# An inference step of a hybrid decoder: last experts' products re-ordered, an eleventh expert piece loaded ahead

## The reference

```python
def mixer_output_and_ffn(x, ya, yb, ym, w_out, g_ffn, w_rg, w_re, w_gate, w_up, w_down):
    mixed = jnp.concatenate([ya..., yb..., ym...], axis=-1)
    h = x + jnp.einsum("bsc,cd->bsd", mixed, w_out)
    return h + hier_moe(rms_norm(h, g_ffn), w_rg, w_re, w_gate, w_up, w_down)

def hier_moe(n, w_rg, w_re, w_gate, w_up, w_down):
    # top-1 of 4 expert groups, then top-2 of 8 experts in that group, softmax over the two
    hg = jnp.einsum("nd,edf->nef", t, w_gate)      # 32 experts, d = 2048, f = 256
    hu = jnp.einsum("nd,edf->nef", t, w_up)
    act = jax.nn.silu(hg) * hu * gates[..., None]
    return jnp.einsum("nef,efd->nd", act, w_down)
```

## Time and profile before

| what | value |
|---|---|
| median of 3 executions | 1140.29 us (1138.39 to 1141.09) |
| the profiled execution's own time | 1141.11 us |
| its span, first to last instruction | 1139.2 us |
| mean granted TensorE clock | 0.985 of full speed |
| TensorE busy (matmul) | 1050.7 us, 92% |
| VectorE busy | 550.0 us, 48% |
| ScalarE busy | 200.1 us, 18% |
| read from HBM | 375.63 MB |

### The profile page before, as it was taken

One profiled execution on the slowest core, in us unless ns is written; L12 is line 12 of the kernel. 1 busy time (PEld: TensorE's weight loads), 2 busy tenths in 40 slices (PEclk: granted clock), 3 DMA queues, 4 the chain that ended last, 5 costly groups with the idle time before them and its releaser, 6 DMA issues.

```text
span 1139.2 us, 17257 instructions
## 1 busy us (share of the span) xinstructions
PE 1050.7 (92%) x7153; PEld 585.5 (51%) x7153; DVE 550.0 (48%) x1079; ACT 200.1 (18%) x457; POOL 41.7 (4%) x39
## 2 busy tenths in 40 slices
PE   8999999999999999999999998999997969787976
PEld 3687776666666676677777442333332313232322
DVE  3775554664455455495442135544443434343423
ACT  1022112221212231312010112121211111111110
POOL 0031010000100000010000000000000000000000
PEclk9999999999999999999999999999999999999997
DMA  9899449899999999724856368999999999999993
GB/s 327 329 287 323 185 142 417 319 372 348 350 409 390 375 358 361 295 97 158 336 201 243 148 267 356 417 425 426 427 427 428 427 429 429 427 429 427 427 427 135
DMA packets 38612, 384.53 MB, mean 338 GB/s; under 512 B 4863, under 2 KB 7551, under 8 KB 10207
## 3 DMA queue, kind: packets, MB, share of 16 engines
q1 hardware_dynamic: 35968, 375.83, 82.1%
q0 software_dynamic: 1568, 5.62, 1.9%
q10 hardware_dynamic: 1008, 2.10, 0.5%
HBM read 375.63 MB, written 7.90 MB: 337 GB/s over the span
## 4 chain that ended last, share of the span: by engine, by line
PE 71%; DMA 16%; DVE 8%; ACT 2%; issue 2%; POOL 1%; SPq 0%; ACTq 0%; DVEq 0%; POOLq 0%
PE ps L605 24%; DMA arena<-w_gu 12%; PE ps L597 7%; PE ps L1024 6%; PE ps L1001 5%; PE ps L1055 5%; PE ps L1039 4%; DMA arena<-w_proj 4%; PE ps L798 4%; PE ps L587 3%; PE ps L765 3%; DVE cst L1802 1%; PE ps L1060 1%; DVE cst L1741 1%; PE ps L781 1%
## 5 line engine op out<-in xcount | busy, mean ns | idle before, releaser
L605 PE MATMUL ps<-arena 128*128 128x256 f32 x1456 | 332.9, 383 | 1.0 <-DVE arena L1345 1.0
L605 PEld LDWEIGHTS ps<-arena 128*128 128x128 f32 x1456 | 270.5, 190 | 51.0 <-issue 14.4
L1024 PE MATMUL ps<-arena,cst 128*32 128x512 f32 x1024 | 122.8, 614 | 32.7 <-DMA arena<-w_gu 31.0
L1802 DVE STREAM_TRANSPOSE cst<-ps 128x512 f32<-128x512 f32 x31 | 22.2, 717 | 173.7 <-PE ps L1001 173.7
L597 PE MATMUL ps<-arena 128*64 128x256 f32 x832 | 101.3, 385 | 0.0
L1001 PE MATMUL ps<-arena,cst 128*32 128x512 f32 (+1 forms) x768 | 94.0, 603 | 0.0
L1024 PEld LDWEIGHTS ps<-arena,cst 128*32 128x32 f32 x1024 | 32.1, 112 | 118.2 <-issue 81.2
L1039 PE MATMUL ps<-arena,stat 128*32 128x512 f32 x512 | 66.6, 640 | 23.8 <-DVE stat L1806 23.8
L597 PEld LDWEIGHTS ps<-arena 128*64 128x64 f32 x832 | 55.1, 136 | 37.8 <-issue 14.2
L1824 DVE COPY arena<-ps 32x512 f32<-32x512 f32 x64 | 44.2, 691 | 45.8 <-PE ps L1039 44.5
L1055 PE MATMUL ps<-arena,cst 128*128 128x512 f32 x128 | 57.0, 598 | 9.4 <-ACT cst L1275 9.4
(11 more groups left out here) (264 smaller groups left out, 978.4 us busy)
## 6 DMA issues: line engine op xcount, KB each, us to landing
arena<-w_gu SPq DMA_DIRECT2D x64, 2048.0 KB, 29.2
arena<-w_dn SPq DMA_DIRECT2D x32, 2048.0 KB, 27.5
arena<-w_proj SPq DMA_DIRECT2D x43, 1024.0 KB, 7.7
arena<-kc SPq DMA_DIRECT2D x16, 2048.0 KB, 10.7
arena<-vc SPq DMA_DIRECT2D x16, 2048.0 KB, 9.4
arena<-w_o SPq DMA_DIRECT2D x16, 1024.0 KB, 4.9
arena<-kc SPq DMA_DIRECT2D x8, 1024.0 KB, 8.3
arena<-vc SPq DMA_DIRECT2D x8, 1024.0 KB, 9.8
```

Source lines behind the costliest of these rows:

```text
L605: last = mm(psum[:, regions(v)[j - 1]], left[a], right[:, a], start=first and opens and a == 0, stop=final and a == 1, skip_group_check=True)
L1024: last = mm(ps[g:g + 32, 0, :], xgT[:, s % 2, kt, :], w[:, k, :], start=kt < 4, stop=kt >= KT - 4)
```

## The change

- The kernel asks for 8192 bytes of dynamic DMA scratch per partition, and `arena` grows from 49152 to 51200 floats per partition, by 8192 bytes.
- Piece 0 gets a place used once, behind the pieces 6 and 7: over the later `y4`, the routing's old scratch and `fresh` (sums of the output projection), which moves to the new end. Its load waits for `h_ready` 9, the last use of `fresh`. The ring's indices shift by one, so pieces 0 to 10 are issued before any piece is used; piece 11 waits for two used pieces, and from 11 on each piece waits for the same count as before.
- The routing's small tensors move to `gv` and to constants no longer used; the comparison `cmpb` is made in two halves through one smaller tensor.
- In the last body the second spreading is re-ordered. The weights' transposes and copies are made in the last block but one (`early_turns`), those of the last block's rows also at the partitions of their tile. Products of the first three blocks of `y4` (96 rows) with tile 0 are made before the last block's rows exist (`early_products`), at three places; `yres` of the small tile is put into PSUM by a product with the identity (`rows_first`). When the last block's rows are there, ScalarE copies them once (`y_last`), four products of 32 rows finish tile 0 (`last_tiles`), the small tile is finished and copied by ScalarE, and tile 1 follows. Each tile is stored in two halves of its columns.

```diff
@@ -132,7 +132,7 @@
...
-ARENA = 49152
+ARENA = 51200
...
@@ -221,13 +221,14 @@
...
-fresh = area(A_S + D + 512, 4, HALF)
-once = {6: A_N2, 7: A_N2 + PIECE}
+A_LATE = A_S + 2 * D
+fresh = area(A_LATE, 4, HALF)
+once = {0: A_S + D, 6: A_N2, 7: A_N2 + PIECE}
...
-    return u if u < 6 else (u - 2) % RING
+    return u - 1 if u < 6 else (u - 3) % RING
...
@@ -238,12 +239,13 @@
...
+y_last = area(A_S, COLS)
+pw_last = area(A_S + COLS, NT)
...
-squares = area(A_S + D, COLS)
...
@@ -278,36 +280,39 @@
...
-R0 = A_S + D
-mx = area(R0, 3, 8)
...
-pickb = area(R0 + 1168, 2, 3, 32)
...
-cmpb = area(R0, NMORE, 32)
...
+squares = part
...
+E0 = A_I + 132
+mx = field(gv, E0, 3, 8)
...
+L0, NPART = done + 6 * P + 512, NMORE // 2
+top = field(cst, L0, 3, 8)
...
+pickb = pick
+cmpb = field(cst, L1, NPART, 32)
...
@@ -530,30 +536,32 @@
...
         if o in (1, 3, 5):
-            piece(o // 2, 0)
+            piece(1 + o // 2, o // 5)
         if o in (7, 9):
...
         if o == 11:
-            piece(3, 1)
+            piece(4, 1)
+    sp.wait_ge(h_ready, 9)
+    piece(0, 0)
     sp.wait_ge(unit_done, UNITS_M + UNITS_X + 45)
-    piece(4, 1)
+    piece(5, 1)
     sp.wait_ge(unit_done, UNITS_M + UNITS_X + 48)
-    piece(5, 1)
     piece(8, 2)
+    piece(9, 3)
     sp.wait_ge(logits, 1)
-    piece(9, 3)
-    for u in range(10, 3 * BODY + 10):
+    piece(10, 3)
+    for u in range(11, 3 * BODY + 11):
         sp.wait_ge(piece_used, u - 9 if u < 16 else u - 7)
...
         for j in range(count):
-            u = j + 10
+            u = j + 11
             if j == 0 or u % 3 == 0:
                 e = sp.value_load(eblk_i[0:1, ds(i * BODY + u // 3, 1)], min_val=0, max_val=NEXP - 1)
-            sp.wait_ge(piece_used, i * (3 * BODY) + (j + 3))
+            sp.wait_ge(piece_used, i * (3 * BODY) + (j + 4))
             if u % 3 < 2:
...
@@ -564,11 +572,22 @@
...
-    pieces(last, 3 * BODY - 10)
-    for t, (r0, m) in enumerate(ROWS):
-        sp.wait_ge(added[t], last * 8 + 8)
-        sp.dma_start(o_y[r0:r0 + m, :], yres[0:m, t]).then_inc(y_stored_out, 16)
-    sp.wait_ge(y_stored_out, 48)
+    pieces(last, 3 * BODY - 11)
+    def store(t, h):
+        r0, m = ROWS[t]
+        cols = slice(h * D // 2, (h + 1) * D // 2)
+        sp.dma_start(o_y[r0:r0 + m, cols], yres[0:m, t, cols]).then_inc(y_stored_out, 16)
+    for h in range(2):
+        sp.wait_ge(added[0], last * 8 + (6 + 2 * h))
+        store(0, h)
+    for h in range(2):
+        sp.wait_ge(small_out, 2 * h + 2)
+        store(2, h)
+    for h in range(2):
+        sp.wait_ge(added[1], last * 8 + (6 + 2 * h))
+        store(1, h)
+    sp.wait_ge(y_stored_out, 96)
...
@@ -1007,15 +1026,65 @@
...
-            pe.wait_ge(ring_loaded[u], 16)
+            pe.wait_ge(ring_loaded[u - 1], 16)
...
-            pe.wait_ge(ring_loaded[(u - 2) % RING], i * 48 + 16 * ((u - 2) // RING + 1))
+            pe.wait_ge(ring_loaded[(u - 3) % RING], i * 48 + 16 * ((u - 3) // RING + 1))
+    def early_turns(i):
+        pe.wait_ge(added[1], i * 8 + 4)
+        pe.wait_ge(added[2], i * 8 + 4)
+        pe.wait_ge(pw_made, i * 2 + 2)
+        for t, (r0, m) in enumerate(ROWS):
+            last = tr(ps[:, 4, r0:r0 + m], pw[0:m, t, :], ident[0:m, 0:m])
+        last.then_inc(pwt_mm, 1)
+        for t, (r0, m) in enumerate(ROWS):
+            for g in range(4):
+                last = mm(ps[32 * g:32 * g + 32, 5, r0:r0 + m], pw[0:m, t, 96:128], ident[0:m, 0:m], start=True, stop=True)
+        last.then_inc(pwl_mm, 1)
+    def early_products(i, ns):
+        for n in ns:
+            mm(ps[:, 4 + n, :], pwT[0:96, 0:P], y4[0:96, 512 * n:512 * n + 512], start=True, stop=False)
+    def rows_first(i, n):
+        for j in range(2):
+            cols = slice(1024 * n + 512 * j, 1024 * n + 512 * j + 512)
+            mm(ps[64 * j:64 * j + 64, 1 - n, :], ident[0:64, 0:64], yres[0:64, 2, cols], start=True, stop=False)
+    def last_tiles(i):
+        pe.wait_ge(yl_ready, 1)
+        for n in range(4):
+            mm(ps[:, 4 + n, :], pw_last[32 * n:32 * n + 32, 0:P], y_last[32 * n:32 * n + 32, :],
+               start=False, stop=True).then_inc(comb_mm, 1)
+        pe.wait_ge(ye_copied, i * (4 * BODY) + 4 * (BODY + 1))
+        for k in range(2):
+            for j in range(2):
+                cols = slice(1024 * k + 512 * j, 1024 * k + 512 * j + 512)
+                last = mm(ps[64 * j:64 * j + 64, 1 - k, :], pwT[:, 2 * P:NT], y4[:, cols], start=False, stop=True)
+            last.then_inc(small_mm, 1)
+        for n in range(4):
+            if n >= 2:
+                pe.wait_ge(added[0], i * 8 + (4 + n - 1))
+            mm(ps[:, 2 + n, :], pwT[:, P:2 * P], y4[:, 512 * n:512 * n + 512], start=True, stop=True).then_inc(comb_mm, 1)
...
+            ends = final and s == BODY - 1
...
+                if final and s == BODY - 2 and h:
+                    early_turns(i)
+                if ends and h:
+                    rows_first(i, 0)
+                    pe.wait_ge(pwl_ready, 1)
+                    pe.wait_ge(pwt_ready, i * 2 + 2)
+                    pe.wait_ge(ye_copied, i * (4 * BODY) + 4 * BODY)
+                    early_products(i, [0])
...
@@ -1026,10 +1095,14 @@
...
                 gather((b + 1) % BATCH, i * 2 + (2 + (s + 1) // BATCH))
+            if ends:
+                early_products(i, [1])
             pe.wait_ge(gu_copied, i * BODY + (s + 1))
...
             last.then_inc(ht_mm, 1)
+            if ends:
+                rows_first(i, 1)
             pe.wait_ge(act_ready, i * BODY + (s + 1))
...
@@ -1039,7 +1112,10 @@
...
             last.then_inc(piece_used, 1)
-            if b < BATCH - 1:
+            if ends:
+                early_products(i, [2, 3])
+                last_tiles(i)
+            if b < BATCH - 1 or ends:
                 continue
...
@@ -1258,14 +1334,29 @@
...
-    def experts(i, first):
+    def experts(i, first, final):
...
+            if final and s == BODY - 2:
+                act.wait_ge(pwt_mm, i * 2 + 2)
+                act.wait_ge(pwl_mm, 1)
+                copy(pwT, ps[:, 4, 0:NT]).then_inc(pwt_ready, 1)
+                copy(pw_last, ps[:, 5, 0:NT]).then_inc(pwl_ready, 1)
...
+            if final and s == BODY - 1:
+                copy(y_last, ps[:, 3, :]).then_inc(yl_ready, 1)
+                act.wait_ge(yl_ready, 1)
+                for g in range(2):
+                    copy(y4[96:128, 512 * g:512 * g + 512], y_last[32 * g:32 * g + 32, :]).then_inc(ye_copied, 1)
+                for n in range(2):
+                    act.wait_ge(small_mm, n + 1)
+                    for j in range(2):
+                        copy(yres[0:64, 2, 1024 * n + 512 * j:1024 * n + 512 * j + 512], ps[64 * j:64 * j + 64, 1 - n, :]).then_inc(small_out, 1)
+                continue
...
@@ -1782,9 +1873,10 @@
...
-    link(V.tensor_tensor(cmpb, incl.unsqueeze(1).to_broadcast([P, NMORE, 32]),
-                         iota[:, 0:NMORE].unsqueeze(2).to_broadcast([P, NMORE, 32]), ALU.is_le))
-    link(V.tensor_reduce(ebf, cmpb, X, ALU.add))
+    for n in (0, NPART):
+        link(V.tensor_tensor(cmpb, incl.unsqueeze(1).to_broadcast([P, NPART, 32]),
+                             iota[:, n:n + NPART].unsqueeze(2).to_broadcast([P, NPART, 32]), ALU.is_le))
+        link(V.tensor_reduce(ebf[:, n:n + NPART], cmpb, X, ALU.add))
...
@@ -1792,6 +1884,12 @@
...
+    def add_tile(ready, t, n, bank, before):
+        dve.wait_ge(comb_mm, ready)
+        cols = slice(512 * n, 512 * n + 512)
+        V.tensor_tensor(yres[:, t, cols], ps[:, bank + n, :], before[:, t, cols], ALU.add).then_inc(added[t], 1)
...
@@ -1819,6 +1917,14 @@
...
+            if final and s == BODY - 1:
+                dve.wait_ge(yl_ready, 1)
+                for g in range(2, 4):
+                    V.tensor_copy(y4[96:128, 512 * g:512 * g + 512], y_last[32 * g:32 * g + 32, :]).then_inc(ye_copied, 1)
+                for t in range(2):
+                    for n in range(4):
+                        add_tile(i * 20 + (10 + 4 * t + n + 1), t, n, 4 - 2 * t, yres)
+                continue
...
@@ -2004,7 +2108,7 @@
...
-    nc = _bacc.Bacc("TRN2", target_bir_lowering=False, num_devices=1)
+    nc = _bacc.Bacc("TRN2", target_bir_lowering=False, num_devices=1, dynamic_dma_scratch_size=8192)
...
```

More of the change, by code:

```diff
@@ L243, in hybrid_step @@
         assert A_N2T + 8 * NT + 3 * P <= A_Y
-        squares = area(A_S + D, COLS)
         y4 = area(A_S + D, D)
-        assert A_S + 2 * D == ARENA and A_N2 + 2 * PIECE == A_S + D
+        assert A_LATE + D == ARENA and A_N2 + 2 * PIECE == A_S + D
         def field(t, at, *dims):
@@ L306, in hybrid_step @@
-        cntf = area(R0 + 1444, 8)
-        cmpb = area(R0, NMORE, 32)
-        ebf = area(R0 + 1452, NMORE)
-        acc = area(R0 + 1452 + NMORE, 3, 32)
-        assert NMORE * 32 <= 848 and 1452 + NMORE + 96 <= D
+        squares = part
+        E0 = A_I + 132
+        mx = field(gv, E0, 3, 8)
+        mi = field(gv, E0 + 24, 3, 8).bitcast(U32)
+        grp = field(gv, E0 + 48, 3, 1)
```

(38 more changed lines are left out.)

10 lines of the change are left out of this document (removed).

## The result

| what | before | changed |
|---|---|---|
| median | 1140.26 us (1134.65 to 1143.17, 10 executions) | 1133.07 us (1131.84 to 1136.99, 10 executions) |
| ratio | 1 | 0.9945, 95% interval 0.993 to 0.996 |
| profiled execution's own time | 1141.11 us | 1135.25 us |
| its span | 1139.2 us | 1133.3 us |
| mean granted TensorE clock | 0.985 | 0.987 |

The change made the kernel faster by 0.4 to 0.7%; the forecast was 1132.8 us. Here are the stretches of the changed kernel: busy us (instructions) of PE, PEld, DVE, ACT and POOL, then TensorE's clock, DMA share and GB/s.

The account below looks back on a forecast made before the run. TensorE's pace bounds the weight stream up to 738.7 us, then the stream itself, then a 27.4 us tail. Eleventh piece and routing nothing, tail 7.5 us: span 1139.2 to 1131.7, execution 1133.6, median 1132.8; range 1129.8 to 1138.0.

Parts of the forecast that it names:

- the test of 19 to 21: Sign: the prediction is wrong if the tail behind the last piece is not 19 to 21 us.
- the other test, 1 us around 1111.8: Sign: the prediction is wrong if the last piece lands more than 1 us from 1111.8.
- The eleventh piece: Weight stream before piece 20's gate: worth nothing, ends 0.9 us gain and 0 loss; rival that it shortens the stream, 0.07.
- Routing and scratch: Routing's split comparison and moved tensors: nothing, some 0.2 us covered; rival that halved scratch holds up POOL, 1147 us, 0.04.
- The tail, step by step: From 1111.82: down products end 1118.7, last add 1127.8, span ends 1131.7 instead of 1139.2, 7.5 us less.
- the base of the sum: Start of the tail's step times: last gate-up products at 1111.82.
- the other bound: Four products of 32 rows finishing tile 0: one after another, 3.6 us, instead of 0.89 together; rival of 0.05.
- The 3.9 us that the sum names for clock and waits: Tail up to the down products: about 3.9 us of the gain from the clock and shorter waits.
- The clock: Tail: filling the wait keeps the upper level, 2.4 GHz; rival that it drops all the same, 1137.8 us, 0.13.
- The stores: Kernel's end: last store issued near 1128, span end 1131.7, the middle of bounds 1132.3 and 1131.1.
- the five stores before: Stores ahead of the last: 2 MB, 4.9 us from 1123.2 on, done before it.
- The formula: Last half store: about 2.0 us fixed plus bytes at 436 GB/s, landing after 3.2 us, sum 1131.6.

Follow-up runs that it names:

- experiment 8: Changed kernel with late first spreading and small tile over 128 partitions: eleven pieces 1131.23 us, ten pieces 1130.91; beside them the changed kernel again, 1133.44.
- Experiments 1: Changed kernel with the ten pieces ahead and release counts of the kernel before (new tail alone): 1132.88 us, ratio to before 0.9936.
- Experiment 2: Changed kernel with the tail, stores and adds of the kernel before (eleventh piece alone): 1138.46 us, ratio to before 1.0004.
- experiments 3: Changed kernel with rows_first and the early product moved behind the last gate-up piece, TensorE idle before it: 1137.45 us, ratio to before 0.9983.
- experiment 5: Changed kernel with three whole stores of y instead of six halves: 1133.18 us, ratio to before 0.9946.
- experiment 4: Kernel before with two unread 128 x 512 products in the wait for the last gate-up piece: 1137.49 us, ratio to before 0.9989.
- the kernel before with the late spreading: Kernel before, first spreading of the first body moved behind the gate-up pieces of block 4: 1136.02 us, ratio to before 0.9981.
- experiments 6: The wide small tile: changed kernel, small tile copied as 128 x 512 and stored in four parts from 128 partitions: 1131.18 us, ratio to before 0.9928.
- experiment 7: First spreading of the first body moved behind block 4's gate-up pieces: in the changed kernel 1132.14 us (0.9927), in the kernel before 1136.02 (0.9981).

## Why the prediction was right, point by point

- **The time.** 1132.8 was forecast and 1133.07 measured. The profiled execution was put at 1133.6 and took 1135.25: 0.5 us of the difference is piece 20, at 739.20 instead of 738.68 (piece 11 came 1.2 us earlier than forecast, then the lower clock fell into the first block, whose down products took 3.59 us at 693.6, and cost 1.7); 1.1 us is the last stores. That the medians agree to 0.3 us is partly luck: the profiled execution stood 2.2 us above its median and not 0.8, and this made up for both terms. The tail, 20.9 us, only just met the test of 19 to 21, and the changed kernel's second profile (experiment 8), with the last gate-up products at 1114.61, would have failed the other test, 1 us around 1111.8; its tail was 20.9 as well.
- **The eleventh piece at nothing.** It was loaded in the hole at 642 to 657 (143 GB/s there), piece 11 was issued at 689.22, a second hole appeared ahead of piece 20, 2.5 us long, and piece 20 came 0.5 us later and not earlier. Experiments 1 and 2 show the worth from both sides, by their traces more sharply than by their medians, and experiment 8 that it is nothing also behind the next gate.
- **Routing and scratch at nothing.** Experiment 2 carries both and is level (its interval leaves room for a loss of 2.9 us). From the last output weights to piece 11 pass 51.1 us both with the moved tensors (the changed kernel and experiments 2, 3 and 5) and with the old ones (experiment 4, and the kernel before with the late spreading). POOL's root behind the eight stores stood idle for the same 13.16 us as in the earlier trace rows, so the smaller scratch held up nothing.
- **The tail, step by step.** From the last gate-up products (1112.37 in this run, 0.55 later than the base of the sum) the down products end at 1119.2 where 1118.7 + 0.55 was forecast; the four products of 32 rows start together and take 1.07 us (0.89 forecast, 3.6 the other bound); the last add ends at 1128.4, forecast 1127.8 + 0.55. That is exact to 0.3 us at each step. Up to the end of the down products 3.0 us less was forecast (1121.74 to 1118.7 from the same start), and 3.1 was measured (9.9 to 6.8 us). The 3.9 us that the sum names for clock and waits does not follow from its own terms: 3.0 with the 0.9 and 0.3 of added work would be 4.2.
- **The clock.** The forecast that filling the wait keeps the upper level held in the profiled execution, and experiments 3 and 4 show it from both sides. Its share was not separated in the prediction's sum from the shorter waits; experiment 4 puts the clock at 2.9 us of the 27.4, with the wait for the last down piece behind it.
- **The stores: the term that was mis-sized.** I took 3.7 us from the last issue to the span's end (1128.0 to 1131.7); with the last issue at 1123.53 + 5.28 - 0.34 = 1128.47 and the end at 1133.3 it was 4.8. I had said that the five stores before would be done; they were not. The DMA share was 0.92 or more from 1126 to 1132.5, but the rate was only 186 GB/s at 1128 to 1130, while the small tile's stores were in flight (experiment 5). That these held up the last one is the reading that fits: with the wide small tile the last issue, at 1127.2, was 4.1 us ahead of the end. The formula that the prediction takes from the Trainium skill (page "DMA: Bandwidth & Descriptors", section "Anatomy of one DMA") gave 3.6 us for this term, landing and end together. The page fits that formula to transfers issued from GpSimd, and these stores are SyncE's.

## What to carry to other kernels

Ahead of a stream with a prefetch, look for the first issue that waits for the consumer in the old and in the new order alike: what was loaded ahead of that gate here showed only as a longer hole in front of it. And where TensorE waits just ahead of its last chain (2.9 us here), try filling the wait, best with work that is due anyway: the chain behind it then ran at the upper clock in all nine profiles.

## What the runs showed of the hardware that I had not expected

- With stores from 64 partitions in flight the DMA share was 0.92 at a rate of 186 GB/s over 2 us (0.94 and 191 in the changed kernel's second profile); with the same rows spread over 128 partitions, in four stores, it was 0.93 at 306.
- The lower clock behind an idle stretch had no fixed length: without fill, behind 2.87 us of idle, a mean of 0.63 over 4.6 us is 3.4 us at the lower level, where the kernel before had 10 us, and behind 2.71 us of idle it came only some 6 us later (experiment 4). I have no explanation for it, and none was tried.
- With eleven pieces ahead and the gate in its old place, piece 20 was issued between 735.1 and 741.6 us (the changed kernel's second profile), and the whole time moves with it. Part of this lies before the experts: the last output weights went out at 635.75 with the eleventh piece alone and at 638.14 in the changed kernel. Another part, 1.7 us, is the lower clock in the first block of the changed kernel (down products of 3.59 instead of 1.92 us, 49.98 instead of 48.28 us from piece 11 to piece 20). This scatter is as large as the gains of experiments 6 and 7, which is why their medians leave them unclear.
